# A key and value layer in rounded products, modulation rows spread over four stages, and gated tiles in 512-column matmuls

## The reference

```
mod  = split(silu(c)     @ w_mod + b_mod, 6)     # shift1, scale1, gate1, shift2, scale2, gate2
modc = split(silu(c_ctx) @ w_mod + b_mod, 6)     # only shift1 and scale1 are used
h  = rms_norm(x)  * (1 + scale1)  + shift1       # 256 tokens
hc = rms_norm(ctx) * (1 + scale1c) + shift1c     # 256 context tokens
glu, q, k, v, z, ab, br = split(h @ w_in)        # hc gives k, v and ab too
u = glu_a * sigmoid(glu_gate)                    # then a depthwise convolution of 31 taps,
                                                 # a layer norm, silu and @ w_conv_out
k, v, q = silu(conv5(...)); a gated delta rule over context and tokens
x = x + gate1 * (...) @ w_out
h = rms_norm(x) * (1 + scale2) + shift2
x = x + gate2 * peer(h)                          # 16384 experts, dense here
```

## Time and profile before

| | |
|---|---|
| median of 3 runs | 4372.63 us (4372.29 to 4376.31) |
| profiled execution | 4372.82 us, span 4371.0 us |
| mean granted TensorE clock | 0.989 of full speed |
| busy: TensorE, VectorE, ScalarE, GpSimd | 97%, 67%, 43%, 5% |
| `first_stage`, its tiles | 117.0 to 306.5 us |
| key and value stage | 308.7 to 762.7 us |
| `query_stage` | 766.6 to 880 us |
| `conv_stage` | 880 to 1040 us |
| `output_stage`, its first 32 tiles | 1623.5 to 1823.5 us |
| `expert_output`, its tiles | 2725.5 to 3429.5 us |

### The profile page before, as it was taken

One profiled execution on the slowest core, in us unless ns is written; L12 is line 12 of the kernel. 1 busy time (PEld: TensorE's weight loads), 2 busy tenths in 40 slices (PEclk: granted clock), 3 DMA queues, 4 the chain that ended last, 5 costly groups with the idle time before them and its releaser, 6 DMA issues. The chain is left out here.

```text
span 4371.0 us, 66652 instructions
## 1 busy us (share of the span) xinstructions
PE 4228.5 (97%) x24335; PEld 3509.9 (80%) x24335; DVE 2926.4 (67%) x5073; ACT 1867.0 (43%) x2817; POOL 222.0 (5%) x532
## 2 busy tenths in 40 slices
PE   8999999999998999999999999999999999999999
PEld 1984444968998889888888888788888788888888
DVE  5549875777687765558876665555555567876746
ACT  1520000454663334444445555444444465454534
POOL 0000000000004630000000000000000100300000
PEclk9999999999999999999999999999999899999999
DMA  9457653437876335456655555666666454444554
GB/s 368 160 202 269 239 219 146 145 124 277 283 235 209 103 100 175 157 195 209 212 196 184 184 183 178 226 216 216 216 216 216 141 188 173 149 160 154 174 193 155
DMA packets 211384, 846.12 MB, mean 194 GB/s; under 512 B 67536, under 2 KB 105696, under 8 KB 122096
## 3 DMA queue, kind: packets, MB, share of 16 engines
q1 hardware_dynamic: 211184, 843.37, 55.8%
HBM read 792.85 MB, written 50.45 MB: 193 GB/s over the span
## 5 line engine op out<-in xcount | busy, mean ns | idle before, releaser
L2569 PE MATMUL bank<-rounded,rounded 128*128 128x512 f32 x2048 | 738.5, 403 | 7.6 <-DVE rounded L2715 7.6
L3397 PE MATMUL bank<-rounded,rounded 128*128 128x512 f32 x1856 | 667.2, 403 | 9.5 <-DVE rounded L3641 6.4
L2571 PE MATMUL bank<-rounded,rounded 128*128 128x256 f32 x2048 | 575.4, 281 | 0.0
L3398 PE MATMUL bank<-rounded,rounded 128*128 128x256 f32 x1856 | 521.1, 281 | 0.0
L290 DVE TENSOR_TENSOR rounded<-arena,rounded 128x1024 fp32r<-128x1024 f32 x255 | 312.4, 1225 | 303.7 <-ACT rounded L283 303.7
L2569 PEld LDWEIGHTS bank<-rounded,rounded 128*128 128x128 f32 x2048 | 386.6, 189 | 95.5 <-issue 8.2
L205 PE MATMUL bank<-arena 128*128 128x512 f32 x1024 | 441.7, 593 | 2.3 <-PEq L101 2.3
L283 ACT ACTIVATE rounded<-arena 128x1024 fp32r<-128x1024 f32 x255 | 270.4, 1061 | 392.3 <-PE bank L2955 385.2
L2623 ACT ACTIVATE rounded<-arena 128x1024 fp32r<-128x1024 f32 x256 | 271.4, 1061 | 372.5 <-PE bank L2571 371.2
L3397 PEld LDWEIGHTS bank<-rounded,rounded 128*128 128x128 f32 x1856 | 349.9, 189 | 99.5 <-issue 13.7
L3641 DVE TENSOR_TENSOR rounded<-arena,rounded 128x1024 fp32r<-128x1024 f32 x230 | 284.3, 1236 | 193.8 <-ACT rounded L3443 192.2
(11 more groups left out here) (499 smaller groups left out, 8839.5 us busy)
## 6 DMA issues: line engine op xcount, KB each, us to landing
arena<-in_w_in SPq DMA_DIRECT2D x244, 1024.0 KB, 4.9
arena<-in_peer_u SPq DMA_DIRECT2D x128, 1024.0 KB, 4.9
arena<-in_peer_v SPq DMA_DIRECT2D x128, 1024.0 KB, 4.9
arena<-in_w_mod SPq DMA_DIRECT2D x96, 1024.0 KB, 6.7
arena<-in_w_out SPq DMA_DIRECT2D x40, 1024.0 KB, 4.9
arena<-in_w_conv_out SPq DMA_DIRECT2D x16, 1024.0 KB, 4.9
arena<-in_w_dn_out SPq DMA_DIRECT2D x16, 1024.0 KB, 4.9
arena<-in_peer_w_q SPq DMA_DIRECT2D x16, 1024.0 KB, 5.7
```

Source lines behind the costliest of these rows:

```text
L2569: pe.matmul(k.ps[r][:], wh, flat(k.r(pair_slot + 2 * kt, 2)), start=(kt == 0), stop=False, skip_group_check=True)
L2571: mm = pe.matmul(k.ps[r][:, 0:L], wl, k.r(pair_slot + 2 * kt, 1)[:, 0, :], start=False, stop=(kt == KT - 1), skip_group_check=True)
L3397: pe.matmul(both, wh, hi_lo(kt), start=(kt == 0), stop=False, skip_group_check=True)
L3398: mm = pe.matmul(one_, wl, hi(kt), start=False, stop=(kt == KT - 1), skip_group_check=True)
```

## The change

- `first_stage`: for each input tile one 512-column matmul (high weights times high and low tokens side by side) and one of 256 columns (low weights times high tokens) replace the three of 256. The two halves of a bank are then joined: ScalarE copies the second half out (`carry`), VectorE adds the first (`join`), ScalarE makes sigmoids of four tiles at once (`open_gates`), VectorE multiplies. It also makes high and low parts of the context tokens (`context_high`, `context_low`), and sums the rows of gate1.
- The new `kv_stage` replaces `linear` with `grid_conv_side`: rounded products of 512 columns. The 30 side taps work in PSUM banks 5 and 7; ScalarE does the middle tap into the bank and copies the sums out. It holds the gate product (rounded, three matmuls per input tile) and the rows of scale2.
- `query_stage`: its first high and low parts are made in the stage before; four moves of 1024 elements on ScalarE; taps begin at half 3.
- `conv_stage`: gate product and the split leave it.
- `output_stage` sums the rows of shift2, `expert_output` those of gate2, 32 steps of 1024 columns, with 16 column sums at its end. The x load of `output_stage` comes in two parts at tiles 6 and 9.

Rows of gate1, scale2 and shift2 are made by one class, `ModRows`: 16 pieces of 1 MB, 64 steps of 512 columns on VectorE, four groups of four one-column matmuls.

```diff
+class ModRows:
+    def load(self, sp, n):
+        if n >= 2:
+            sp.wait_ge(self.stepped, 4 * (n - 1))
+        sp.dma_start(self.piece(n), self.k.i["w_mod"][self.first + n]).then_inc(self.piece_in[n % 2], 16)
+    def step(self, dve, m):
+        k, c, kt = self.k, m // KT, m % KT
+        if m % 4 == 0:
+            dve.wait_ge(self.piece_in[(m // 4) % 2], 16 * (m // 8 + 1))
...
+            dve.wait_ge(self.stepped, m)
+            ins = dve.scalar_tensor_tensor(out=self.total(c), in0=rows, scalar=gate, in1=self.total(c), op0=ALU.mult,
+                                           op1=ALU.add)
+    def columns(self, pe, c):
+        pe.wait_ge(self.stepped, KT * (c + 1))
+        for m in range(4):
+            mm = pe.matmul(self.bank[:, 4 * c + m:4 * c + m + 1], self.total(c)[:, m * P:(m + 1) * P],
+                           self.k.ones[:, 0:1], start=True, stop=True)
...
 first_stage:
+    ROW_AT = [8 + m * 52 // 64 for m in range(64)]
-                    pe.matmul(out, wh, hi, start=(kt == 0), stop=False)
-                    pe.matmul(out, wh, lo, start=False, stop=False)
-                    mm = pe.matmul(out, wl, hi, start=False, stop=(kt == KT - 1))
+                    pe.matmul(both_, wh, k.halves(k.quad(kt), 0, 2), start=(kt == 0), stop=False, skip_group_check=True)
+                    mm = pe.matmul(one_, wl, k.x_part(0, kt), start=False, stop=(kt == KT - 1), skip_group_check=True)
...
+                if i % 2:
+                    join(i // 2 - 1)
+                    if i // 2 - 1 >= 16:
+                        glu(i // 2 - 17)
+                if 21 <= i < 21 + KT:
+                    context_low(i - 21)
+                for m in range(64):
+                    if ROW_AT[m] == i:
+                        gate1.step(dve, m)
+            low(tiles, 0)
+            join(31)
             glu(15)
+            gate1.finish(dve, 32)
...
+def kv_stage(k, w, following):
+    conv_by = lambda i: CONV * min(i + 1, 62) // 62
+    row_by = lambda i: ROWS * min(i + 1, 60) // 60
...
+                    pe.matmul(out, wh, k.both_tokens(0, kt), start=(kt == 0), stop=False)
+                    pe.matmul(out, wh, k.both_tokens(1, kt), start=False, stop=False)
+                    mm = pe.matmul(out, wl, k.both_tokens(0, kt), start=False, stop=(kt == KT - 1))
+                mm.then_inc(k.half_done, 1)
+                if i == 5:
+                    gate_product()
...
+            def tap(n):
+                g, m, a = n // (2 * TAPS), n % (2 * TAPS) // 2, n % 2
+                t, shift = 2 * g + a, taps[m] - middle
+                if m == 0:
+                    dve.wait_ge(first_tap, 2 * g + 2)
+                else:
+                    dve.wait_ge(conv_step, n - 1)
...
+                dve.scalar_tensor_tensor(out=o, in0=x, scalar=tap_at(t, taps[m]), in1=o, op0=ALU.mult,
+                                         op1=ALU.add).then_inc(conv_step, 1)
...
+            for i in range(halves + 1):
+                if i > 0:
+                    low(i // 2, i % 2)
...
+                while taps_done < conv_by(i):
+                    tap(taps_done)
+                while rows_done < row_by(i):
+                    rows.step(dve, rows_done)
...
-CONV_AT = [i for i in range(32) for _ in range(1 if 6 <= i < 14 else 2 if i < 24 else 3)][:10 * V_FIRST]
+CONV_AT = [i for i in range(32) for _ in range(0 if i < 3 else 1 if 6 <= i < 14 else 2 if i < 21 else 3)][:10 * V_FIRST]
...
 conv_stage:
-                if j == 0:
-                    gate_product()
-            for q in range(4):
-                dve.wait_ge(split_high, q + 1)
-                dve.tensor_tensor(k.r(32 + 4 * q, 4), k.t(32 + 4 * q, 4), k.r(48 + 4 * q, 4), ALU.subtract).then_inc(split_low, 1)
...
 expert_output, after the last tile:
+            pe.wait_ge(kept2, 2)
+            pe.wait_ge(row_added, groups)
             for m in range(KT):
+                mm = pe.matmul(k.ps[5][:, m:m + 1], row_sums[m // 8][:, (m % 8) * P:(m % 8 + 1) * P], k.ones[:, 0:1],
+                               start=True, stop=True)
+            mm.then_inc(rows_summed, 1)
+            for m in range(KT):
+                if m == 5:
+                    pe.wait_ge(gate_set, 1)
```

More of the change, by code:

```diff
@@ L476, in _ @@
                     side_sync(sp)
-            load_next(k, sp, following, None, s + tiles)
+                for n in range(16):
+                    if j == (3 + n if n < 2 else (ROW_AT[4 * n - 5] + 5) // 2):
+                        gate1.load(sp, n)
+            load_next(k, sp, None, following, s + tiles)
         @block.gpsimd
@@ L580, in _ @@
                     context(i - 2)
-                if i % 2 and i // 2 - 1 < 16:
-                    evacuate(i // 2 - 1)
+                if 20 <= i < 20 + KT:
+                    context_high(i - 20)
+                if i % 2:
+                    carry(i // 2 - 1)
+                if i % 8 == 4 and 12 <= i < 44:
+                    open_gates((i - 12) // 8)
+            carry(tiles - 1)
         @block.vector
@@ L916, in _ @@
                     out = k.ps[j % 4][:, 0:L]
-                    pe.matmul(out, wh, hi(kt), start=(kt == 0), stop=False)
-                    pe.matmul(out, wh, lo(kt), start=False, stop=False)
-                    mm = pe.matmul(out, wl, hi(kt), start=False, stop=(kt == KT - 1))
+                    if j == 1 and kt == 8:
+                        pe.wait_ge(moved, 4)
+                    hi, lo = ((k.x_part if j == 0 else k.kept_x_part)(part, kt) for part in range(2))
+                    pe.matmul(out, wh, hi, start=(kt == 0), stop=False)
+                    pe.matmul(out, wh, lo, start=False, stop=False)
+                    mm = pe.matmul(out, wl, hi, start=False, stop=(kt == KT - 1))
                 mm.then_inc(k.half_done, 1)
@@ L1122, in sums @@
                     pe.matmul(out, one_row(h), flat(square(n)), start=(h == 0), stop=(h == HEADS - 1)).then_inc(summed, 1)
-            def gate_product():
-                pe.wait_ge(wab_in, 16)
-                for kt in range(KT):
-                    mm = pe.matmul(k.out(4, 2 * L)[0:64], wab[:, kt, :], k.hx(kt), start=(kt == 0), stop=(kt == KT - 1))
-                mm.then_inc(product, 1)
             def gate_turn():
@@ L2285, in output_stage @@
         carried = sem("carried")
+        rows = ModRows(k, sem, "shift2", 48, 132, 148, k.ps[7])
+        ROW_AT = [8 + m * 52 // 64 for m in range(64)]
         block = stage.enter_context(nc.Block())
@@ L2293, in _ @@
                 sp.dma_start(k.raw(j % 2), w(j)).then_inc(k.raw_loaded[j % 2], 16)
+                for n in range(16):
+                    if j == (3 + n if n < 2 else (ROW_AT[4 * n - 5] + 5) // 2):
+                        rows.load(sp, n)
+                if j in (6, 9):
+                    c = 8 * (j // 9)
+                    sp.dma_start(k.t(x_slot + c, 8), k.i["x"][:, c:c + 8]).then_inc(x_in, 16)
                 if j in (36, 38, 40, 42):
@@ L2351, in _ @@
                 mm.then_inc(k.half_done, 1)
+                for c in range(4):
+                    if i == ROW_AT[KT * c + KT - 1] + 2:
+                        rows.columns(pe, c)
                 if 37 <= i < 64 and i % 2:
@@ L2449, in _ @@
                     merged_low((i - 4) // 2)
+                for m in range(64):
+                    if ROW_AT[m] == i:
+                        rows.step(dve, m)
+                if i == 62:
+                    rows.finish(dve, 48)
                 if i % 2 and 35 <= i < 67:
@@ L2881, in expert_output @@
     nc = k.nc
+    rows, row_sums = flat(k.t(48, 4)), [flat(k.t(52 + 4 * m, 4)) for m in range(2)]
+    b0 = COL_AT["b_mod"][0] + 80
     s = k.raws
```

494 lines of the change are left out of this document (272 added, 222 removed).

## The result

The changed kernel took 4310.9 us (median of four runs, 4304.6 to 4313.1) against 4372.5 us (4369.2 to 4376.3) of the kernel before: a ratio of 0.9857 (95% interval 0.9839 to 0.9874), 61.6 us less. The forecast was 87.8 us less, 4285 us, in a range of 4268 to 4308. So the direction held, and the time lies 3 us above the range. The profiled execution took 4311.9 us, its span 4310.1.

The account below looks back on a forecast made before the run. TensorE, busy 97% of the span, was taken as the bound, so only its matmuls or gaps before them count. Stage terms summed to -87.8 us, from 4372.8 to 4285 us, with an 8-in-10 range of 4268 to 4308.

Parts of the forecast that it names:

- key and value stage: Rounded 512-column products replace plain fp32, taps hidden, 2.7 us for the start: 369.5 us against 454.0, -84.5 us.
- first stage and the gap behind it: First stage: cheaper matmuls, added row sums and crowded halves, +2.6 us; longer wait at its end, +1.3 us.
- into the query stage, and the stage: Shorter gap before the query stage with the clock kept, -4.3 us; later taps and silu keeps within it, +1.5 us.
- convolution output stage: Gate product leaves, saving 13.95 us, less 1.6 for late key squares: -12.3 us (bounds -14 and -8).
- output stage: Row sums on TensorE, +3.7 us, and three crowded odd halves, +0.9: +4.6 us (to +10).
- expert output, tiles: Expert output stage: 32 row steps on VectorE and 16 MB more transfers hidden within 704 us, no cost.
- expert output, behind the tiles: End of expert output stage: 16 row sums before the first gated addition, +3.3 us (0 to +4); clock may be kept.
- three to a half ... +0.3: Query stage: taps packed three to a half over the last 11 halves; 8 halves at issue against 7, +0.3 us.
- about 148: Sign to look for: the convolution output stage lasting about 148 us.
- stalls on VectorE in the crowded stages: Rival, chance 0.18: late low parts in first, query and output stages, +18 us (4303), or taps of 0.55 us (4325).
- Better than counted: Rival, chance 0.11: the fixed 0.011 us per matmul gone in the key and value stage, -17 us, 4268 us.
- VectorE as the key and value stage's bound: Rival "slower", chance 0.03: PSUM taps wait for their own writes; at 0.75 us a tap, stage 475 us, kernel 4390.

Follow-up runs that it names:

- y3_taps: Changed kernel with the 30 side taps of the key and value stage's convolution done twice; 4414.1 us (one run), that stage 471.8 us.
- x4_between: Changed kernel with each group's gate2 row step in the expert output stage moved between the two low parts of the group's last tile; 4302.2 us, ratio to before 0.9838.
- y4_behind: x6_spread with the gate2 row step put back behind the second low part, as in the changed kernel; 4294.6 us, ratio to before 0.9818.
- x5_parts: x4_between with each 512 KB transfer of gate2 rows cut into three, one behind the weights of each of three tiles; 4292.1 us, ratio to before 0.9811.
- y2_onepiece: Changed kernel loading only the first two 1 MB row pieces in first, key and value and output stages, all steps and sums kept; 4303.7 us (one run).
- x6_spread: x5_parts with the 2 MB of saved tokens cut into sixteen 128 KB parts over the first sixteen groups; 4294.6 us, ratio to before 0.9822.
- x2_steps: Changed kernel with all gate2 row steps in the expert output stage but one transfer of rows instead of 32; 4303.0 us (one run).
- x3_moves: Changed kernel with all 32 gate2 row transfers in the expert output stage but no row steps on VectorE; 4310.4 us (one run).
- z2_whole: x6_spread with the gate2 column sums in the bank that VectorE copies first, row pieces of the other stages left whole; 4287.2 us, ratio to before 0.9800.

## Why the prediction missed, point by point

| term | forecast | measured |
|---|---|---|
| key and value stage | -84.5 | -87.2 |
| first stage and the gap behind it | +3.9 | +4.8 |
| into the query stage, and the stage | -2.8 | +2.3 |
| convolution output stage | -12.3 | -10.1 |
| output stage | +4.6 | +4.6 |
| expert output, tiles | 0 | +19.1 |
| expert output, behind the tiles | +3.3 | +6.5 |
| all else | 0 | -1.0 |
| sum (profiled executions) | -87.8 | -61.0 |

The query row runs from the end of the key and value stage to the next stage's first matmul (122.5 us before, 124.8 now). The rows of the output stage and of the expert output tiles run from start to start, as in the tables above.

**Key and value stage: right.** 366.8 us to a forecast sum of 366.8, to which 2.7 us for the start were added. Rounded 512-column products cost what the same form cost elsewhere, and taps that write a PSUM bank are hidden. VectorE sets the stage only when the taps are doubled (y3_taps). At the start TensorE waited once, 2.2 us, for the low part (bound 0 to 5). That wait is within the 366.8 us, so the other terms together came out about 2 us too high.

**Expert output stage: the step that failed** is "32 row steps of 1024 elements (1.2 us) in 704 us where VectorE is busy 397.7: hidden; 16 MB more transfers, hidden". For the steps it was argued from a mean over the stage, VectorE busy 56% of it, and for the transfers no reason was given. What counts is one tile of 5.5 us. ScalarE is ready for the next weights 5.7 us after their issue, and they land after 4.9, or after 6.0 when 512 KB of rows are ahead of them; and a step of 1.28 us does not fit in 0.85 idle ones. Of the +19.1 us, 13.6 are in tiles 9 to 128. There, moving the step gave back 2.5 (x4_between; 5.8 once the transfers are in parts, y4_behind), and cutting the transfers 10.4 more (x5_parts). 2.7 us are in tiles 2 to 8, where the wait for weights at the start grew from 3.9 to 5.2 us: one transfer of rows now stands there with the 2 MB of saved tokens that stood there before. With the rows in parts and the tokens spread these tiles took 6.1 us less, 2.5 less than in the kernel before. The last 2.8 us are in tile 1 and are the clock's, not the row work's: it fell there in the changed kernel and not in the kernel before, behind the same idle time.

The first and output stages were priced by what fits in a half; the output stage came out as forecast (+4.6). The same sum was not made for the stage that looked idle in the mean.

**Behind the tiles.** The forecast put 1.3 us to the second copy, 3.7 for the sums and 0.6, which it gives as 5.7 us (they add up to 5.6); x4_between is close to that (5.9, sums 3.87). In the changed kernel the clock fell during the sums, so that they took 5.7 us (1.00 up to 3364.0, 0.50 from there):

```profile
3362.56 5.72 PE L3069 MATMUL bank<-cst,arena 128*128 128x1 f32 x32 [1.38 <-DVE arena L3177]
3368.13 2.37 PE L3083 MATMUL bank<-cst,arena 128*128 128x128 f32 x10
```

The forecast's "TensorE then is less idle there and may keep its clock" fell: the clock was at 0.50 for 34 us from there, where it was 27 in the kernel before. This stretch is the rest of the +6.5; the gated addition itself comes 5.3 us later.

**Query stage.** The shorter gap came as forecast: TensorE's idle time before its first matmul went from 3.87 us to 1.88. But the clock did not stay: it is 0.50 from 684.5 to 687.5 (windows above). Besides, TensorE waits more in the middle of the stage. Its waits in the changed kernel:

```profile
PE bank L987 <- ACT arena L1013: 2.8, 1, 2.8
PE bank L987 <- DVE rounded L1053: 2.8, 3, 1.8
```

Leaving out the gap, these are 5.6 us, where the kernel before had 2.3. The four moves on ScalarE have no part in it: they were done by 690.6, and the waits come from 723.3 on, the longest at 767.4. The first row names the evacuation (L1013) only because it ended last before TensorE started; the bank of that tile had been free since 748.7. What came late is the low part:

```profile
765.62 0.49 DVE L926 TENSOR_SCALAR arena<-arena 128x512 f32<-128x512 f32 x1 [3.70 <-ACT arena L1018]
766.02 1.22 DVE L1053 TENSOR_TENSOR rounded<-arena,rounded 128x1024 fp32r<-128x1024 f32 x1
767.39 0.36 PE L987 MATMUL bank<-rounded,rounded 128*128 128x256 f32 x1 [2.83 <-ACT arena L1013]
```

Its high part was ready at 763.0, but the low part stood in VectorE's queue behind the first tap of a pair, which waited 3.7 us for a keep on ScalarE (L1018). So here the forecast's "three to a half ... +0.3" was too small: it counted VectorE's work and not what a tap waits for. No run changed this order; it is read from the trace alone.

**Convolution output stage.** 142.4 us against "about 148" in the list of signs, a slip there: 152.5 less the forecast 12.3 is 140.2. TensorE waits 1.0 us for the key squares, as forecast (0.9 to 1.9). The 2.2 us over are about what the clock took: it was at 0.50 for 5.3 us at the stage's start and 3.4 us from 872.3, against 2.9 us in all in the kernel before. Matmuls at half pace for 5.8 us more cost 2.9 us at the most (an estimate from these lengths).

**The first stage** came out 2 us over its +2.6. Leaving out the row pieces' transfers gave 1.6 back (y2_onepiece, one execution), again a cost that the forecast had at nothing.

Of the rivals, "stalls on VectorE in the crowded stages" is nearest to the measured time, but not by its mechanism: the stalls are in the stage that was not crowded, and most of them begin at the DMA queue. "Better than counted" and VectorE as the key and value stage's bound are refuted.

## What to carry to other kernels

Whether added work is hidden is asked of one period of the pipeline, not of the stage: the free time of the engine at the very place in its queue, and for a transfer the time between a landing and its first use. A transfer that shares the weights' queue should be cut to a size that fits in that slack, here a third or so of 512 KB at each of three tiles; where the consumer itself waits for the piece, as in the first stage, cutting only makes it later. Large loads that are needed late (2 MB of saved tokens) should not stand ahead of weights that are needed now. And before a difference of 3 us in a stage is read, its first tile is looked at alone: the clock can put as much there by itself.

## What the runs showed of the hardware

TensorE's clock does not follow from the length of a gap alone. The step from the key and value stage to the query stage is the same code in x5_parts and x6_spread, with 2.27 us between the last matmul start of one and the first of the other stage. The granted clock of the following stretch, first x5_parts, then x6_spread, whose last matmul started at 683.71:

```profile
682.70:697.70 15.00, 15.00 (x106) 14.38 (x107) 5.98 (x7) 8.26 (x9) 0.00 (x0) 1.00 0.41 141
```

```profile
685.98:700.98 15.00, 15.00 (x95) 14.43 (x96) 4.48 (x6) 8.26 (x9) 0.00 (x0) 0.89 0.36 121
```

In the kernel before, a gap of 2.2 us kept the clock, and the forecast took that for a rule. It was one draw: with the same gap the clock stayed at its upper level (2.4 GHz) once and went to the lower (1.2 GHz) for a few microseconds the other time. Of the thirteen profiled executions other than the kernel before's, six kept it at the start of the query stage and seven lost it. At the start of the expert output tiles, behind 2.8 us of idle time in every kernel, the first tile took 5.5 to 5.6 us in the kernel before, x2_steps, x3_moves and y4_behind, 8.3 to 8.4 in the changed kernel, x6_spread and z2_whole, and 6.9 to 7.2 in the others. The sums behind the tiles (3.73 to 5.78 us for sixteen) show the same.

An operation of VectorE that reads and writes a PSUM bank showed no price over one in SBUF. The 480 taps, in and out of a bank, have a median of 448 ns, where the same taps in SBUF had 442 in the kernel before. From start to start, tap behind tap, it is a median of 0.36 us in both (418 pairs and 240). First the changed kernel, then the kernel before:

```profile
L817 DVE SCALAR_TENSOR_TENSOR bank<-arena,bank x480: 417/448/481, 315.1 to 663.2; 128x200 f32<-128x200 f32 x16, 128x212 f32<-128x212 f32 x16, 128x224 f32<-128x224 f32 x16, 128x236 f32<-128x236 f32 x16
```

```profile
L733 DVE SCALAR_TENSOR_TENSOR arena<-arena x480: 409/442/480, 317.0 to 721.4; - x140, 128x200 f32<-128x200 f32 x2, 128x212 f32<-128x212 f32 x2, 128x224 f32<-128x224 f32 x2
```

The Trainium skill's page "VectorE: DVE Perf Modes" (section on the TRN2 errata) gives PSUM a larger fixed cost; by it, as an estimate, a tap would have been 0.065 us longer than in SBUF. The measured durations do not show that.
